# Index and gate tables of an expert unit: sixteen small TensorE products and one copy each, in place of sixteen VectorE blocks

## What is computed

```python
s = jnp.einsum('thpc,hpnc->thpn', q, subkeys)
sv, si = lax.top_k(s, PEER_TOPK)
cand = (sv[:, :, 0, :, None] + sv[:, :, 1, None, :]).reshape(blk, PEER_HEADS, 256)
cidx = (si[:, :, 0, :, None] * N_KEYS + si[:, :, 1, None, :]).reshape(blk, PEER_HEADS, 256)
fv, fi = lax.top_k(cand, PEER_TOPK)
eidx = jnp.take_along_axis(cidx, fi, axis=-1)
gate = jax.nn.softmax(fv, axis=-1)
act = gelu(einsum('thkd,td->thk', pu[eidx], xb)) * gate
out = einsum('thk,thkd->td', act, pv[eidx])
```

## Time and profile before

| | us |
|---|---|
| median of three runs | 2066.74 |
| the profiled execution | 2056.84 |
| its span | 2055.0 |
| TensorE products busy | 1449.9 |
| VectorE busy | 1503.8 |
| ScalarE busy | 665.4 |
| GpSimd busy | 782.7 |
| granted TensorE clock, mean of the span | 0.796 |

### The profile page before, as it was taken

How to read it: one execution, slowest core, us unless ns; L and a number is a source line. 1 busy time by engine, 2 the same in 40 slices (tenths; PEclk the granted TensorE clock), 3 DMA queues, 4 the chain that set the end, 5 groups by cost and what they waited for, 6 DMA issues and landing times.

```text
span 2055.0 us, 27759 instructions
## 1 busy us (share of the span) xinstructions
PE 1449.9 (71%) x8692; PEld 793.9 (39%) x8692; DVE 1503.8 (73%) x3930; ACT 665.4 (32%) x1990; POOL 782.7 (38%) x581
## 2 busy tenths in 40 slices
PE   6999988887975886566588576657856675656334
PEld 4445556565653552332345244324523441110001
DVE  4346776555389887778988786888879788887875
ACT  2111222122133442324345232334433333432232
POOL 0277741212024443344334334443434344434341
PEclk9998999988987997777689777868977886556555
DMA  7486758947679999999999999999999999999997
GB/s 303 134 305 222 251 187 290 336 162 233 259 284 402 381 405 423 413 422 418 381 337 379 421 416 423 418 385 362 377 414 417 422 413 376 415 409 421 419 409 303
DMA packets 130912, 726.74 MB, mean 354 GB/s; under 512 B 17121, under 2 KB 19042, under 8 KB 58438
## 3 DMA queue, kind: packets, MB, share of 16 engines
q0 software_dynamic: 75024, 545.82, 65.4%
q1 hardware_dynamic: 55741, 179.15, 23.9%
HBM read 715.92 MB, written 9.09 MB: 353 GB/s over the span
## 4 chain that ended last, share of the span: by engine, by line
DVE 29%; PE 27%; DMA 27%; issue 7%; SPq 4%; ACT 4%; POOL 2%; DVEq 0%; POOLq 0%; ACTq 0%
PE bank L509 26%; DMA RING<-in_peer_uv,R 18%; DVE RING L2375 8%; DMA R<-in_peer_uv,R 6%; DVE R L2384 5%; DVE R L2336 3%; SPq L2631 2%; DVE R L2375 2%; SPq L2687 1%; ACT R L1446 1%; DMA R<-in_x_prompt 1%; DVE R L2284 1%; PE bank L516 1%; DVE R L2106 1%; DVE R L2330 1%
## 5 line engine op out<-in xcount | busy, mean ns | idle before, releaser
L2617 POOL DMA_INDIRECT RING<-in_peer_uv,R x390 | 461.5, 1183 | 760.2 <-PE bank L509 619.6
L509 PE MATMUL bank<-RING,R 128*32 128x512 f32 (+1 forms) x1560 | 302.7, 834 | 387.4 <-ACT R L1446 384.1
L2375 DVE SCALAR_TENSOR_TENSOR RING<-RING,MV 128x1024 f32<-128x1024 f32 x384 | 465.1, 1221 | 141.9 <-DMA RING<-in_peer_uv,R 127.0
L509 PE MATMUL bank<-R 128*128 128x128 f32 (+5 forms) x2184 | 343.9, 423 | 106.7 <-ACT R L1446 101.0
L509 PEld LDWEIGHTS bank<-R 128*128 128x128 f32 (+4 forms) x2184 | 239.1, 188 | 239.7 <-issue 224.5
L1456 ACT ACTIVATE R<-R 128x2 f32<-128x2 f32 x256 | 51.9, 203 | 752.8 <-DVE RING L2375 658.6
L509 PEld LDWEIGHTS bank<-RING,R 128*32 128x32 f32 (+1 forms) x1560 | 40.9, 124 | 519.2 <-issue 508.1
L2375 DVE SCALAR_TENSOR_TENSOR R<-R,MV 128x1024 f32<-128x1024 f32 x128 | 156.3, 1221 | 57.5 <-DMA R<-in_peer_uv,R 55.6
L2617 POOL DMA_INDIRECT R<-in_peer_uv,R x130 | 128.6, 989 | 174.3 <-PE bank L509 154.2
L509 PE MATMUL bank<-R,ident 128*32 128x512 f32 (+6 forms) x548 | 171.3, 594 | 4.5 <-ACT R L1418 2.6
L509 PEld LDWEIGHTS bank<-HT,R 128*128 128x128 f32 x992 | 135.2, 217 | 61.4 <-issue 61.4
(11 more groups left out here) (332 smaller groups left out, 1830.2 us busy)
## 6 DMA issues: line engine op xcount, KB each, us to landing
R<-in_peer_wq SPq DMA_DIRECT2D x12, 2048.0 KB, 12.4
RING<-in_w_mod SPq DMA_DIRECT2D x11, 2048.0 KB, 8.7
R<-in_cache_v SPq DMA_DIRECT2D x84, 256.0 KB, 3.7
MV<-in_cache_k SPq DMA_DIRECT2D x64, 256.0 KB, 3.9
R<-in_cache_k SPq DMA_DIRECT2D x64, 256.0 KB, 3.7
R<-in_w_out SPq DMA_DIRECT2D x6, 2048.0 KB, 15.1
MV<-in_cache_v SPq DMA_DIRECT2D x44, 256.0 KB, 4.0
RING<-in_peer_uv,R POOLq DMA_INDIRECT x390, 11.0
```

Source lines behind the costliest of these rows:

```text
L509: i = nc.tensor.matmul(out, lhsT, rhs, start=start, stop=stop, **k)
L2375: V.scalar_tensor_tensor(u, u, 1.0, QUARTER[s_ % 4], ALU.mult, ALU.mult, accum_out=DOT[:, n % 4, s_:s_ + 1]).then_inc(S("dots"), 1)
L2617: nc.gpsimd.indirect_dma_start(UV[g % UN], None, a["peer_uv"][0], bass.IndirectOffsetOnAxis(ap=idx, axis=0)).then_inc(S(f"uv_in{g % UN}"), 16)
```

## The change

For units 2 to 31 the last piece of the picks writes the indices as floats to a table `NUMBERS` in one operation. At event 5 of the unit ahead, after its slot, TensorE turns the table by sixteen products with columns of the identity (`quarter_turn`) into a bank of ring `D`; VectorE copies the bank to `EIX` after dot 6 and signals `indexed`, for which the unit's first gather waits. For units 1 to 31 `gate_scale` scales the gates in place in one operation; TensorE turns them at event 9, VectorE copies them to `GATS` after dot 10 and signals `gates_scaled`. Units 0 and 1 keep the blocks for the indices, unit 0 for the gates. `sample_sums` moves from unit 29, step 6, to unit 28, step 12.

```diff
+        NUMBERS = R1[:, 12088:12104]
...
+            def quarter_turn(job, src):
+
+                b = take_bank(job, "D")
+                for q in range(4):
+                    for to in range(4):
+                        mm(b[32 * to:32 * to + 32, q:16:4], ident[:, 32 * q:32 * q + 32], src[:, to:16:4], sem=full(job) if q == to == 3 else None)
+
...
+                if m is not None and m < SAMPLES and x == 5 and 0 < m < UNITS - 1:
+                    pe.wait_ge(S("picked"), m + 2)
+                    quarter_turn(("numbers", m + 1), NUMBERS)
+                if m is not None and m < SAMPLES and x == 9 and m < UNITS - 1:
+                    pe.wait_ge(S("gates_whole"), m + 1)
+                    quarter_turn(("gates", m + 1), GAT[:, (m + 1) % 4, :])
...
+                if paired == 2:
+                    step(V.scalar_tensor_tensor(NUMBERS, R01[rows, 0, :], float(NKEY), R01[rows, 1, :], ALU.mult, ALU.add))
+                    return
...
-                yield from picks(P, QT[:, 2 * h:2 * h + 2, 0:P], FVS[:, x, :], EIX[:, x, :], True, n == 0)
+                yield from picks(P, QT[:, 2 * h:2 * h + 2, 0:P], FVS[:, x, :], EIX[:, x, :], 2 if n > 1 else 1, n == 0)
...
+            def indices(n):
+
+                b = full_bank(dve, ("numbers", n))
+                V.tensor_copy(EIX[:, n % 4, :], b[:, 0:16]).then_inc(free(("numbers", n)), 1)
+                job_read(dve, ("numbers", n))
+                dve.sem_inc(S("indexed"), 1)
+
+            def gates_turned(n):
+
+                b = full_bank(dve, ("gates", n))
+                V.tensor_copy(GATS[:, n % 4, :], b[:, 0:16]).then_inc(free(("gates", n)), 1)
+                job_read(dve, ("gates", n))
+                dve.sem_inc(S("gates_scaled"), 1)
...
+                if n:
+                    V.tensor_scalar(GAT[:, x, :], GAT[:, x, :], SUMG[:, x:x + 1], None, ALU.mult).then_inc(S("gates_whole"), 1)
+                    return
                 for a_, b, dst, src_ in blocks:
...
+                    if s_ == 6 and 0 < n < UNITS - 1:
+                        indices(n + 1)
                     if s_ == 8 and n + 1 < UNITS:
                         gate_scale(n + 1)
+                    if s_ == 10 and n + 1 < UNITS:
+                        gates_turned(n + 1)
...
+                    if n == 28 and s_ == 12:
+                        sample_sums()
                     if n == 29:
-                        if s_ == 6:
-                            sample_sums()
-                        elif s_ == 7:
+                        if s_ == 7:
...
-                elif s_ == (0 if n else 8) and n != SAMPLES:
+                elif s_ == (0 if n else 8) and n < 2:
                     pool.wait_ge(S("picked"), n + 1)
+                elif s_ == 0 and n != SAMPLES:
+                    pool.wait_ge(S("indexed"), n - 1)
```

## The result

The kernel after takes 2014.0 us (median of three runs, 2011.07 to 2017.94) where the one before took 2066.74. The ratio of the two is 0.975, with a 95% interval of 0.972 to 0.978: 2.5% faster, 52.7 us, more than four times the forecast 12 and far outside the range from 2041. The profiled execution took 2011.07 us with a span of 2009.2, against 2056.84 and 2055.0. The profiled execution of before lies 10 us under its median, so the two profiles differ by 45.8 us and the medians by 52.7.

A forecast was written before the change was run, and what follows sets the result against it. DMA was taken to bound the expert part, with dips behind VectorE's blocks. 18 us won, less 2.5 for products and 3.5 for handoffs, gave 12 us: 2054.7 us from 2066.74, range 2041 to 2069.

The forecast's parts named there:

- the ceiling of the first part: Expert part, 594 to 2027 us: DMA busy share 0.99 against at most 1.01, so 28 us can be won.
- eight dips: Pieces between 640 and 1730 us with DMA share under 0.98, each with a VectorE block inside or shortly ahead; 21.9 us.
- my ten stretches and the four pieces: Eight low-share stretches of 21.9 us, two with TensorE busy (4.5 and 1.8), four pieces of 0.94 to 0.97, some 2 us.
- of the 21.9 us only 18 are won: Stops shrink from 3.1 or 4.2 to 0.6 us, but VectorE's other load in the dips stays; 18 us won.
- the 2.5 us charged for new products in such stretches: TensorE-busy stretches (600 to 610, 1030 to 1090, 1400 to 1460): added products cost up to 5 us; half charged.
- Rival D: All dips go, also where TensorE is busy: 20 to 28 us won, about 2043 us; chance 0.17.
- VectorE's work: Index and gate blocks removed, 76 and 112 us saved; VectorE's busy time falls about 190 us, to 1310 to 1335.
- The turns: Sixteen TensorE products per table, 61 tables: 0.8 us each, 49 us in all; bounds 0.5 and 6.4 us.
- The handoff: VectorE waits for TensorE's products after dots 6 and 10: 1 us at some six handoffs, 3.5 us beyond the 2.5.
- Rival A: Dips come from the sum of other VectorE work and shrink little: 0 to 4 us less, say 2065; chance 0.21.
- Rival B: VectorE stands at handoffs where TensorE is behind, up to 3.78 us each: 11 us slower, 2078 us; chance 0.09.
- Rival C: TensorE's weight loads and products run one by one, 6.4 us a table: 2087 us; chance 0.03.

The follow-up runs named there:

- the dummies put back: Kernel after with thirty-two small VectorE operations per unit back at steps 0 and 8, writing spare columns nobody reads: 2073.1 us, ratio 1.0032.

## Why the prediction was wrong

The mechanism was right: VectorE's blocks hold back dots, values, buffers and gathers in this order, and DMA runs under its rate for a while. The sign was right, and most marks named ahead came: GpSimd's waits at 669, 1032 and 1405 and the dips around 1000, 1030, 1380 and 1400 are gone, and a table is done within 1 us. GpSimd's waits of 7 us and more for TensorE, from 600 to 1970, went from 30 to 9. What failed is the size of one term.

**The step that failed is the ceiling of the first part**: "the missing time, (1.01 - share) x length", with 28 us as the whole and 21.9 in eight dips. The busy share is not a rate. The earlier trace rows alone says it: 402 of 421 GB/s over 1433 us are 65 us missing (58 against the 419 of its second line), where 0.99 of 1.01 are 28. The kernel before has 137 pieces of 10 us between 600 and 1970; by share they miss 35 us in all, by rate 64.6, and after the change 9.8 and 13.8. My own rows carried both columns: 640 to 680 has a share of 0.91, which I took for 4.0 us, and 353 of 421 GB/s, which is 6.5; the eight dips are 33.6 us by rate. More lay in pieces that my bound of 0.98 never let me see, in some of which VectorE is busy nine tenths (windows of before):

```profile
710.00:740.00 30.00, 27.30 (x160) 17.00 (x160) 24.46 (x70) 13.81 (x42) 12.99 (x12) 0.89 0.99 384
1070.00:1080.00 10.00, 6.74 (x42) 3.90 (x44) 9.34 (x33) 2.76 (x8) 1.88 (x2) 0.93 0.98 342
1090.00:1100.00 10.00, 10.00 (x64) 6.21 (x63) 9.42 (x32) 4.49 (x14) 5.78 (x5) 1.00 0.98 355
1460.00:1470.00 10.00, 10.00 (x69) 6.57 (x67) 9.25 (x34) 4.48 (x14) 5.90 (x6) 1.00 0.98 356
```

A share of 0.98 can stand for a rate 19% short. Cut in 40 slices of 0.25 us, the piece from 1070 to 1080 shows the hole that the one number hides, 98 GB/s at a share of 0.2 to 0.4 in the eleventh to thirteenth slice:

```profile
DMA  8999999999342879899898999665888996899989
GB/s 360 426 426 393 393 393 426 393 361 131 98 98 98 229 328 393 360 393 459 360 492 328 393 295 229 262 262 229 360 360 360 459 361 262 360 360 492 459 360 459
```

Why the share of the whole piece stays at 0.98 is open. In the fourteen profiles the time follows the missing rate closely, as it must where the same bytes are moved (it checks the account and shows no cause): 13.8, 23.8, 36.5, 47.7, 64.6 and 75.3 us missing go with profiled executions of 2011, 2028, 2037, 2048, 2057 and 2072 us. Had I taken the rate in the first table, the ceiling would have been about 65 us. The missing rate fell by 51 us of it, the profiled executions by 45.8 and the medians by 52.7. By share as well my sum was short: my ten stretches and the four pieces add up to 30 us and all pieces to 35, not 28.

A second step failed with it: that of the 21.9 us only 18 are won, because the rest of VectorE's load in the dips stays. All eight dips went, and so did the one from 1050 to 1070, which I had set aside as TensorE's own; the 2.5 us charged for new products in such stretches did not show. TensorE is as full there in the kernel after (19.1 of 20 us) at 422 GB/s, so that it was full was not the cause of that dip. I read it as TensorE catching up after a stop, which no run tests by itself. The dip at 600 stayed and is not explained by the blocks. Rival D had the most of this, at 0.17 and too small by the same ceiling.

**The other terms.** VectorE's work: 190 us less expected, 171 measured, and its total of 1332.7 lies in the 1310 to 1335 named. I took 3.08 and 4.22 us a unit from stretches of the time line, which hold gaps between the operations; by the means of the earlier trace rows, 160 and 244 ns, sixteen are 2.6 and 3.9 us busy. The scaling takes 0.26 us and not 0.17. The turns: 0.8 us a table expected, 0.43 to 0.44 measured:

```profile
1010.17 0.35 PEld L510 LDWEIGHTS bank<-R,ident 128*32 128x32 f32 x32
1010.17 0.44 PE L510 MATMUL bank<-R,ident 128*32 128x4 f32 x32
...
1012.31 0.16 DVE L2404 COPY R<-bank 128x16 f32<-128x16 f32 x1
```

The entry says x32 where the code has 16 products, and the group of all tables x1952 for 976. A product of this kernel leaves two records, so the row of 64 in the earlier trace rows is 32 products at 60 ns. Sixteen like those would be 1.0 us, and the tables take less than half of it: my lower bound of 0.5 us was no bound, as the row was misread by a factor of two and its products have 128 moving columns in place of four. The handoff: 6 us charged in the two points together, no gain from leaving it out (2017.5 without turns against 2014.0). Rival A fell with the dummies put back. Rival B's wait exists, but showed only with fourfold turns. Rival C, the rule of the Trainium skill (TensorE: Matmul & The Clock Gate, Part 3, The mechanism) on loads and products that touch the same rows, would have made a table 6.4 us by my durations. It took 0.44, with the records of the loads (0.35 us) inside it, so by these records the rule does not hold here. The section itself also lets a load run ahead when it goes to the background weight buffer; the trace does not show which buffer these use.

I also took the length of a stop for its whole price. The runs split it: about half of the gain comes with the work, about half with its lying in blocks, and part of the second half depends on whether a block lies at an even or an odd step.

## What to carry to other kernels

Where transfers set the pace, measure what is missing in bytes per second against the best long stretch, not in busy share, and over all pieces, not only over the visible dips. Before taking an engine's work away, try to spread it: here the same operations in fours over four events won 30 of the 53 us. If a consumer takes results in pairs, try a block of other work between two pairs: here it won 11 us for one of two blocks and 5 for the other.

## What the runs showed of the hardware

In pieces of 10 us with a DMA share of 0.98 in the windows' column, 342 to 395 GB/s were moved, while long stretches at 1.01 stand at 419 to 422. Sixteen products of 128 rows by 32 columns with four moving columns each, over four strips of 32 output rows, take 0.43 us with their weight loads (at 1038.6 and 1049.2), at a granted clock of 1.00 (2.4 GHz) in the window from 1030 to 1050. VectorE's sixteen operations of 32x4 took 3.0 to 4.7 us for the same move, where one operation of 128x16 takes 0.16 to 0.26. One `scalar_tensor_tensor` took 160 ns for 32x4 and 176 ns for 128x16, one `tensor_scalar` 244 and 262: at these sizes the cost is by the instruction, not by the element.
